# Down products of four feed-forwards: two row tiles of block 0 ahead of block 1, and block 1's banks asked for later

## What is computed

```python
def _swiglu(h, w_gate, w_up, w_down):
    return (jax.nn.silu(h @ w_gate) * (h @ w_up)) @ w_down      # [256,1024] -> [256,2816] -> [256,1024]

for l in range(2):
    mod = jax.nn.silu(c) @ w_mod[l] + b_mod[l]                  # 9 x 1024 columns: sh, sc, g
    h = _rmsnorm_2(x) * (1.0 + sc1) + sh1
    x = x + HALF_STEP * g1 * _swiglu(h, ffn1_w_gate[l], ffn1_w_up[l], ffn1_w_down[l])
    h = _rmsnorm_2(x) * (1.0 + sc2) + sh2
    x = x + g2 * _hybrid_mixer(h, ...)
    h = _rmsnorm_2(x) * (1.0 + sc3) + sh3
    x = x + HALF_STEP * g3 * _swiglu(h, ffn2_w_gate[l], ffn2_w_up[l], ffn2_w_down[l])
```

## Time and profile before

| | |
|---|---|
| median of 3 runs | 1657.89 us (1656.09 to 1664.91) |
| profiled execution, as a whole | 1658.01 us |
| its span, first to last instruction | 1656.0 us |
| mean granted clock of PE | 0.972 of full speed |
| busy: PE, DVE, ACT, POOL | 1532.7, 1033.0, 677.6, 252.4 us |

### The profile page before, as it was taken

One profiled execution on the slowest core, in us unless ns is written; L12 is line 12 of the kernel. 1 busy time (PEld: TensorE's weight loads), 2 busy tenths in 40 slices (PEclk: granted clock), 3 DMA queues, 4 the chain that ended last, 5 costly groups with the idle time before them and its releaser, 6 DMA issues.

```text
span 1656.0 us, 19267 instructions
## 1 busy us (share of the span) xinstructions
PE 1532.7 (93%) x7584; PEld 1144.4 (69%) x7584; DVE 1033.0 (62%) x1534; ACT 677.6 (41%) x1094; POOL 252.4 (15%) x251
## 2 busy tenths in 40 slices
PE   7997999989889999999989999899988999989999
PEld 1646556546778878775558877788877865477887
DVE  0477695753578887445358886587885553376554
ACT  2415321234255543451245553455533531255652
POOL 0231263003101100052001110011100240001100
PEclk9998999989999999999999999999999999999999
DMA  9443334341368879232347787388886323367551
GB/s 343 146 145 127 102 103 153 117 152 75 129 205 281 263 282 334 94 102 99 105 163 256 252 290 283 116 265 265 306 306 203 128 77 102 118 208 229 195 197 58
DMA packets 192257, 305.28 MB, mean 184 GB/s; under 512 B 6171, under 2 KB 116519, under 8 KB 192039
## 3 DMA queue, kind: packets, MB, share of 16 engines
q1 hardware_dynamic: 189248, 299.45, 53.4%
q10 hardware_dynamic: 2919, 4.61, 0.8%
HBM read 302.99 MB, written 1.05 MB: 184 GB/s over the span
## 4 chain that ended last, share of the span: by engine, by line
PE 68%; DVE 15%; ACT 7%; issue 3%; POOL 2%; DMA 1%; SPq 0%; DVEq 0%; ACTq 0%; POOLq 0%
PE ps L398 67%; DVE accs L539 3%; DVE wlo L2026 2%; ACT whi L1975 2%; DMA ring<-in_ffn_w_down_dram 1%; PE ps L401 1%; DVE H L2049 1%; DVE H L1862 1%; DVE arena L1235 1%; DVE arena L1232 1%; ACT hh L1980 0%; DVE arena L1221 0%; ACT arena L1499 0%; DVE ring_r L1621 0%; POOL arena L2407 0%
## 5 line engine op out<-in xcount | busy, mean ns | idle before, releaser
L398 PE MATMUL ps<-hh,whi 128*128 128x512 f32 x1408 | 493.9, 402 | 26.5 <-DVE hh L2032 21.1
L2026 DVE TENSOR_TENSOR wlo<-ring,whi 128x1024 fp32r<-128x1024 f32 x264 | 323.6, 1230 | 172.0 <-ACT whi L1975 163.4
L1975 ACT ACTIVATE whi<-ring 128x1024 fp32r<-128x1024 f32 x264 | 273.4, 1054 | 270.5 <-PE ps L398 237.8
L398 PE MATMUL ps<-hh,wlo 128*128 128x256 f32 x1408 | 371.2, 284 | 0.0
L398 PEld LDWEIGHTS ps<-hh,whi 128*128 128x128 f32 x1408 | 257.3, 190 | 80.7 <-DVE hh L2032 21.9
L398 PEld LDWEIGHTS ps<-hh,wlo 128*128 128x128 f32 x1408 | 269.4, 191 | 17.1 <-issue 1.7
L398 PE MATMUL ps<-ring,H 128*128 128x512 f32 (+1 forms) x544 | 241.0, 595 | 11.2 <-ACT arena L2170 5.5
L539 DVE SCALAR_TENSOR_TENSOR accs<-ring,misc,accs 128x512 f32<-128x512 f32 x266 | 204.8, 770 | 2.6
L398 PEld LDWEIGHTS ps<-ring,H 128*128 128x128 f32 x544 | 103.9, 197 | 121.4 <-issue 106.1
L398 PE MATMUL ps<-H,ring 128*128 128x256 f32 (+1 forms) x576 | 157.4, 432 | 2.1 <-DVE H L1862 1.1
L398 PE MATMUL ps<-whi,ahi 128*128 128x512 f32 x352 | 141.7, 403 | 8.3 <-DVE H L2049 8.3
(11 more groups left out here) (319 smaller groups left out, 1496.0 us busy)
## 6 DMA issues: line engine op xcount, KB each, us to landing
ring<-in_w_mod_dram SPq DMA_DIRECT2D x84, 1024.0 KB, 7.2
ring<-in_w_in_dram SPq DMA_DIRECT2D x48, 1024.0 KB, 5.1
ring<-in_ffn_w_gate_dram SPq DMA_DIRECT2D x44, 1024.0 KB, 5.6
ring<-in_ffn_w_up_dram SPq DMA_DIRECT2D x44, 1024.0 KB, 5.5
ring<-in_ffn_w_down_dram SPq DMA_DIRECT2D x44, 1024.0 KB, 6.1
ring<-in_w_out_dram SPq DMA_DIRECT2D x12, 1024.0 KB, 4.8
gates<-in_b_mod_dram SPq DMA_DIRECT2D x7, 512.0 KB, 6.6
ring<-in_w_proj_a_dram SPq DMA_DIRECT2D x2, 1024.0 KB, 6.0
```

Of the source, the lines that this page charges most:

```text
L398: return self.e.matmul(o, lhsT, rhs, start=start, stop=stop)
L1975: a.done(a.e.activation(hi, M.slot(key)[:, r0:r0 + rn, :], ACT.Copy), ("whi", l, sub, n))
L2026: v.done(v.e.tensor_tensor(lo, M.slot(key)[:, r0:r0 + rn, :], plain(hi), ALU.subtract), ("split", l, sub, n), *([M.freed(key)] if ends els ...
```

## The change

The down stage asks for block 0's two banks alone. It takes row tiles 0 and 1 as one part, all of block 0 (12 matmuls) before block 1 (12 matmuls), and asks for block 1's banks when its first product comes. Within block 1 of this part tile 0 comes before tile 1. Tiles 2 to 17 and the last four are in the order of before. The steps of `work` on PE that stood behind tiles 0 and 1, two each, stand behind tile 1, four in all. ACT, DVE, POOL and SP have the same code as before.

```diff
-    bs = [[pe.bank(("d", l, sub, blk, hf), "down") for hf in range(2)] for blk in range(2)]
-    for k0 in range(19):
-        part = [k0] if k0 < 18 else [18, 19, 20, 21]
+
+    bs = [[pe.bank(("d", l, sub, 0, hf), "down") for hf in range(2)]]
+    for part in [[0, 1]] + [[k0] for k0 in range(2, 18)] + [[18, 19, 20, 21]]:
         pe.wait_ge(("alo", l, sub, part[-1]))
-        for blk, kt, hf in [(0, k_, h_) for k_ in part for h_ in range(2)] + [(1, k_, h_) for h_ in range(2) for k_ in part]:
+        ahead = [(0, k_, h_) for k_ in part for h_ in range(2)]
+        for blk, kt, hf in ahead + ([(1, k_, h_) for h_ in range(2) for k_ in part] if part[-1] == 21 else [(1, k_, h_) for _, k_, h_ in ahead]):
+            if blk == len(bs):
+                bs.append([pe.bank(("d", l, sub, 1, h_), "down") for h_ in range(2)])
             n, c, s = 44 + kt, slice(blk * 128, blk * 128 + 128), slice(hf * 512, hf * 512 + 512)
             hi, lo = piece(M, n, 1024)
             pe.wait_ge(("split", l, sub, n))
             ins = pe.mm3(bs[blk][hf], (M.AHI[:, kt, c], M.ALO[:, kt, c]), (hi[:, 0, s], lo[:, 0, s]), kt == 0, kt == 21)
             if kt == 21 or (blk and hf):
                 pe.done(ins, *([("staged", l, sub, n)] if blk and hf else []), *([("d", l, sub, blk, hf)] if kt == 21 else []))
-        if k0 < 18:
-            tick(work, 2)
+        if part[-1] < 21:
+            tick(work, 2 * len(part))
     run(work)
```

## The result

The changed kernel takes 1664.0 us (median of 20 runs, 1658.0 to 1668.7) against 1656.36 us (20 runs, 1650.0 to 1664.9). The ratio is 1.0042, with a 95% interval of 1.0031 to 1.0053. That is 7.6 us more where 0.9 us was forecast, and above the upper end of the range, 1663.0. The forecast stood on a median of 3 runs of the kernel before, 1657.89; over 20 runs that median is 1.5 us lower. The profiled execution took 1666.22 us, with a span of 1664.4 us.

The account below looks back on a forecast made before the run. TensorE, busy 93% of the span, was taken as the bound, so time is won only where it stands still. -0.8 (F1) + 1.36 (F2) + 0.76 (F3) - 0.42 (F4) = +0.9 us, giving 1658.9 us; range 1654.0 to 1663.0 us.

Parts of the forecast that it names:

- PE's start: Down stages of feed-forwards F1 to F4: PE starts 2.36, 0, 0.60 and 0.42 us earlier, 3.38 us in sum.
- it doesn't do what it says: Rival: F2's block 0 holds the late bank; with other bank holders F1 or F3 lose their gain too, 1659.7 us; chance 0.10.
- The late release of tile 0: Down stage: row tile 0 released at matmul 18 instead of 12, 1.36 us later from PE's start, delaying DVE's tile 4.
- F1's 0.8 us: First feed-forward's down stage: DVE goes straight from tile 3 to tile 4, gaining 0.8 us, not 2.36.
- the low stretch behind F1's start: Low clock at 598 to 603 in the first feed-forward: should go with its wait, but gives nothing back.
- Ticks: PE's two modulation steps behind tile 0 move behind tile 1: costed at nothing, one sum of 1.05 us if uncovered.
- The clock: TensorE's granted clock behind the lengthened waits of F1 to F3: cost 0 to 1.7 us, taken as 0.
- the longer idle at 1204.40 (2.86 us): PE's idle before F3's down stage in the old kernel: clock stayed 1.00 behind it, so the clock cost was taken as 0.
- F2's low stretch: Second feed-forward: a low clock behind the sum at 1008.40 would lie in the 1.90 us of idle at 1019.62.
- F1's fall: Low clock at 615 to 620 behind F1's first sum (0.66): there already, can only stay.
- slower, by the clock: Rival: longer waits for DVE's sum in F1 to F3 make the clock fall, 1660.6 to 1662.3 us; chance 0.25.
- Faster, in full: Rival: PE's start alone counts, 3.38 us plus 1.7 us for the low stretch behind F1's start, 1652.9 us; chance 0.15.

Follow-up runs that it names:

- e1: Changed order of products, but both blocks' banks asked for at the start as in the kernel before: 1664.2 us, 1.0045 of the kernel before.
- e4: Kernel before, with useless matmuls filling PE's waits ahead of the first up product, the down stage and the first and last modulation sums: 1650.3 us, 0.9938 of before.
- e5: Changed kernel, with useless matmuls filling PE's waits ahead of the first up product, the down stage and the first and last sums: 1653.1 us, 0.9961 of before.
- e3: Changed kernel, with useless matmuls filling PE's waits for the first modulation sum in the down stages of F1 to F3: 1660.2 us, 1.0015 of the kernel before.
- e12: Changed kernel, with useless matmuls filling only the waits for the first and last modulation sums: 1659.0 us, 1.0009 of the kernel before.
- e2: Kernel before in its old order, with block 1's banks asked for only at its first product: 1655.2 us, 0.9990 of the kernel before.
- e13: Kernel before, with useless matmuls filling only the waits for the first and last modulation sums: 1655.7 us, 0.9989 of the unfilled kernel before.
- e9: Kernel before in its old order, with the late bank request and the feed-forwards' modulation sum one row tile later: 1650.7 us, 0.9962 of the kernel before.
- e11: Kernel before in its old order, with late bank request, later modulation sum and useless matmuls filling PE's longest waits: 1642.1 us, 0.9915 of the kernel before.

## Why the prediction was wrong

**PE's start: right.** 595.20 where 595.23 was forecast; F3 gained 0.57 us (0.60), F4 0.41 us (0.42), F2 nothing. The banks are held as counted, so the rival "it doesn't do what it says" fell.

**The late release of tile 0: right.** The sums came 0.78 us earlier, 1.36 and 0.70 us later, counted from the adds. e1 has this loss alone, 3.8 us at the full clock (4.1 expected).

**F1's 0.8 us: right in this trace, wrong in kind.** The first add itself came 0.58 us later in F1 than before, by a down load that ACT waited for a little longer; against it the chain won 0.78 us. But e4 and e5 show that the kernel before would have had this time too at a full clock. The forecast said of the low stretch behind F1's start that it lies ahead of the DVE chain and gives nothing back; the 0.8 us that it counted for the chain were just what this stretch had cost.

**Ticks: right.** No wait shows at the sum that was moved (in F1 at 601.03 us, behind tile 1).

**The clock: this is the step that failed.** It read "cost 0 to 1.7 us. I take 0, as the longer idle at 1204.40 (2.86 us) cost none". The cost was that of 12.6 us of added low time: 4.5 us by the rate of 0.36, 6.3 us at most. Three things were wrong in it. I took one trace in which a wait of 2.86 us left the clock alone as a rule, though the same trace had falls behind waits of 1.07 and 2.19 us; over 20 and 30 runs the kernel with the longer waits has 12.6 us more low time, and filling those waits took most of it away (e3, e12). I let F2's low stretch vanish in the idle time of its last sum, but it came behind that sum (1022 to 1027, in both traces), where nothing takes it up; behind the first sum there was none. And I counted F1's fall as there already, but behind 4.6 us of idle the clock was low from the first matmul on and longer (0.50 over 614 to 619, against 0.72 in the kernel before over the same stretch).

The rule of the Trainium skill ("TensorE: Matmul & The Clock Gate", section "HAM oscillation — how this bites in real kernels"), that a wait ahead of each group of matmuls starts the next group at the lower clock, was named beside this step and given no weight in the sum. The traces agree with it at the first sums of F1 (4.60 us, then 0.50) and F3 (2.77 us, then 0.66), and not at that of F2 (2.39 us, then 1.00).

The rival "slower, by the clock" named the mechanism and the place. Its price, 1.7 to 3.4 us on top of the forecast, was too small by 2.8 us or so, since it priced one or two stretches of 3.4 us where low time grew by nearly four (12.6 / 3.4); the upper end of the range, 1663.0, was set by two. "Faster, in full" fell with the result, and even e2, which doesn't pay for the late release, gains only 1.5 us on median.

**What stays open.** Why the clock falls behind the last sum of F2 in the changed kernel, whose wait there isn't longer. It does so in both of its traces and in e3, and not where that wait is filled (e5, e12); but e1, in which PE takes F2 in the same order and waits as long (1.88 us), shows no fall there. Open too is what makes the 3.3 us between e12 and e13, where the chain alone has 1.4 us.

## What to carry to other kernels

Before an engine is started earlier, look for its next wait: if another engine's chain sets that, the gain turns into idle time, and on TensorE idle time can cost twice, as the next matmuls may run at half pace. A reordering that finishes a unit of work later delays everyone who waits for that unit; here six matmuls, 1.36 us in each stage, cost 3.8 us at the full clock, and the three shortened waits gave 3.3 us back. And where the clock matters, compare low time and span x clock over many runs, not the falls in one trace, and take from the runs themselves what a us of low time costs.

## What the runs showed of the hardware

Matmuls that compute nothing, laid into waits, made this kernel faster: 7.3 us less for the kernel before (e4), 8.6 us between e9 and e11. A stretch of 5 us with a granted clock of 0.66 has 3.4 us of low time and loses 1.7 us at most; in the mean over the program a us of low time cost 0.36 us. Where such stretches fall changes from one execution to the next of the same kernel, and the changed kernel's 20 runs spread over 10.7 us (1658.0 to 1668.7), those with a clock of 0.974 near 1658 and those with 0.966 near 1669.
